# Three sets of expert weights in turn, sample rows first, last sums in the banks

## The reference

```
mix = merged @ w_o
x1  = layer_norm(ALPHA * x + mix)
logits = x1 @ w_group, x1 @ w_router      # top 1 of 4 groups, top 2 of its 8 experts
for each expert e, for the rows routed to it:
    h = silu(xb @ e_gate[e]) * (xb @ e_up[e])
    y = h @ e_down[e]
y = layer_norm(ALPHA * x1 + gate1 * y_first + gate2 * y_second)
```

## Time and profile before

| | us |
|---|---|
| three runs | 1352.65, 1344.41, 1345.07 |
| median | 1345.07 |
| the profiled execution | 1349.2 |
| its span, first to last instruction | 1347.4 |
| TensorE busy | 1120.7 (83%) |
| VectorE busy | 442.2 (33%) |
| ScalarE busy | 238.4 (18%) |
| POOL busy | 113.5 (8%) |

### The profile page before, as it was taken

One profiled execution on the slowest core, in us unless ns is written; L12 is line 12 of the kernel. 1 busy time (PEld: TensorE's weight loads), 2 busy tenths in 40 slices (PEclk: granted clock), 3 DMA queues, 4 the chain that ended last, 5 costly groups with the idle time before them and its releaser, 6 DMA issues.

```text
span 1347.4 us, 21857 instructions
## 1 busy us (share of the span) xinstructions
PE 1120.7 (83%) x9267; PEld 779.1 (58%) x9267; DVE 442.2 (33%) x817; ACT 238.4 (18%) x413; POOL 113.5 (8%) x97
## 2 busy tenths in 40 slices
PE   7999989998989989998999827898878778777730
PEld 4888867777678878876864324444434434444410
DVE  5200013775647657333323262111111111111137
ACT  4000010244321111120101101212111111111101
POOL 0300000000000000000001101111111111111104
PEclk9999999999999999997999958999999999999975
DMA  9432242222221012164454056899999999999941
GB/s 326 134 123 78 68 142 79 63 71 70 55 59 47 27 50 59 26 212 149 169 211 176 32 219 275 365 426 424 424 426 425 423 428 425 425 426 424 414 193 63
DMA packets 48477, 290.82 MB, mean 216 GB/s; under 512 B 9491, under 2 KB 11605, under 8 KB 35594
## 3 DMA queue, kind: packets, MB, share of 16 engines
q1 hardware_dynamic: 43234, 281.41, 53.6%
q0 software_dynamic: 5184, 8.54, 1.7%
HBM read 274.98 MB, written 24.23 MB: 222 GB/s over the span
## 4 chain that ended last, share of the span: by engine, by line
PE 62%; DMA 24%; DVE 6%; ACT 3%; issue 2%; DVEq 2%; POOL 0%; POOLq 0%; SPq 0%; ACTq 0%
PE psum L692 60%; DMA arena<-in_e_up 22%; DVE arena L1477 3%; PE psum L697 2%; ACT arena L1234 2%; DVE arena L1480 2%; DMA arena<-in_p_abm 0%; DMA arena<-in_w_in 0%; DVEq L2099 0%; POOL arena L2112 0%; DVEq L2044 0%; DMA arena<-scratch_x,arena 0%; DMA arena<-in_w_mem_kv 0%; DVE arena L1495 0%; DVEq L1496 0%
## 5 line engine op out<-in xcount | busy, mean ns | idle before, releaser
L692 PE MATMUL psum<-arena 64*64 64x64 f32 (+8 forms) x8760 | 1054.9, 337 | 153.0 <-ACT arena L1234 36.3
L692 PEld LDWEIGHTS psum<-arena 64*64 64x64 f32 (+4 forms) x8760 | 725.3, 151 | 461.6 <-issue 159.4
L1477 DVE TENSOR_TENSOR arena<-arena,psum 128x256 f32<-128x256 f32 (+3 forms) x136 | 74.6, 549 | 504.1 <-PE psum L692 359.5
L1234 ACT ACTIVATE arena<-psum 128x512 f32<-128x512 f32 (+11 forms) x144 | 88.2, 635 | 807.8 <-PE psum L697 413.6
L1477 DVE TENSOR_TENSOR arena<-arena 128x1024 f32<-128x1024 f32 (+17 forms) x168 | 129.8, 784 | 32.6 <-PE psum L692 8.0
L697 PE MATMUL psum<-arena 128*128 128x128 f32 (+5 forms) x507 | 73.9, 279 | 21.3 <-DMA arena<-scratch_x,arena 7.1
L697 PEld LDWEIGHTS psum<-arena 128*128 128x128 f32 (+5 forms) x507 | 54.2, 145 | 53.4 <-issue 31.8
L2112 POOL TENSOR_TENSOR arena<-arena 128x1024 f32<-128x1024 f32 (+1 forms) x15 | 40.9, 2735 | 508.9 <-DVE arena L1477 508.9
L2157 POOL DMA_INDIRECT arena<-scratch_x,arena x32 | 34.0, 1063 | 414.8 <-DVE arena L2060 363.6
L1477 DVE TENSOR_TENSOR arena<-psum,arena 128x256 f32<-128x256 f32 (+4 forms) x85 | 47.1, 565 | 65.7 <-PE psum L692 61.5
L1480 DVE SCALAR_TENSOR_TENSOR arena<-arena 128x520 f32<-128x520 f32 (+7 forms) x72 | 47.1, 667 | 11.1 <-DMA arena<-scratch_ya 7.1
(11 more groups left out here) (111 smaller groups left out, 186.5 us busy)
## 6 DMA issues: line engine op xcount, KB each, us to landing
arena<-in_e_gate SPq DMA_DIRECT2D x32, 2048.0 KB, 26.0
arena<-in_e_up SPq DMA_DIRECT2D x32, 2048.0 KB, 26.5
arena<-in_e_down SPq DMA_DIRECT2D x31, 2048.0 KB, 26.0
arena<-in_w_in SPq DMA_DIRECT2D x46, 512.0 KB, 4.0
scratch_gates<-arena SPq DMA_DIRECT2D x24, 260.0 KB, 4.2
arena<-scratch_gates SPq DMA_DIRECT2D x8, 780.0 KB, 4.7
arena<-in_p_abm SPq DMA_DIRECT2D x8, 640.0 KB, 5.8
scratch_x<-arena SPq DMA_DIRECT2D x8, 512.0 KB
```

The costliest lines, as they stand in the source:

```text
L692: return pe.matmul(out, a, b, start=start, stop=stop)
L1234: return act.activation(out, a, ACT.Copy)
L1477: return v.tensor_tensor(out, a, b, op)
```

## The change

Four edits.

1. Expert weights: sets 0, 1 and 2 take turns for all 32 experts. SP's waits become those of three sets, and its down loads for set 2 are four DMAs. TensorE's loop has six experts in its body instead of two.
2. Output projection: the samples' tile is first (`tile_at` now holds for pas 1 too). Its two halves of 512 columns go to rows 0 to 7 and rows 64 to 71 of bank 0, alternating. VectorE moves the upper half to rows 0 to 7 with one more copy and adds in two operations.
3. The last sums: VectorE scales the identity with each of the two gates for the four prompt tiles (`dg`, eight operations, made before the experts). At the end TensorE puts x1 into all eight banks by products with the identity, and adds the two entries of each row by products with these diagonals. VectorE's statistics and ScalarE's scaling read from the banks. The samples' tile stays on VectorE.
4. The last layer norm's offset moves from POOL to VectorE.

```
-            return (t - 1) % Q if pas == 2 else t
+            return (t - 1) % Q if pas else t
...
-            def gate_load(e, q, done):
-                sp.wait_ge(s["gate_mm"], done + 3)
+            def gate_load(e, q):
+                sp.wait_ge(s["gate_mm"], e)
...
+            def down_load(e, q):
+                sp.wait_ge(s["y_mm"], e)
+                if q < 2:
+                    sp.dma_start(ed[q], one(wd, e)).then_inc(s[f"ew{q}d_in"], 16)
+                else:
+                    for k in range(FF // P):
+                        sp.dma_start(ed2[k], one(wd, e)[:, k, :]).then_inc(s["ew2d_in"], 16)
...
-            gate_load(4, 1, 1)
-            down_load(3, 0, 0)
-            up_load(4, 1, 1)
-            gate_load(5, 0, 3)
-            down_load(4, 1, 1)
-            up_load(5, 0, 3)
-            with sp.Fori(0, NE // 2 - 3) as i:
-                for q in (1, 0):
-                    e = i * 2 + (7 - q)
-                    gate_load(e, q, e - 2)
-                    down_load(e - 1, 1 - q, e - 3)
-                    up_load(e, q, e - 2)
...
+            with sp.Fori(0, NE // 3 - 1) as i:
+                for j in range(3):
+                    e = i * 3 + (4 + j)
+                    gate_load(e, (1 + j) % 3)
+                    down_load(e - 1, j)
+                    up_load(e, (1 + j) % 3)
...
+                    if t == NT:
                         for c in range(KD):
-                            last = mm(bank(2 * (t % 2) + h, 512)[0:n, :], MG[:, c, t * P:t * P + n], wo[h][:, c, :], c == 0, c == KD - 1)
+                            for h in range(2):
+                                last = mm(bank(0, 512)[h * 64:h * 64 + B, :], MG[:, c, T:N], wo[h][:, c, :], c == 0, c == KD - 1)
...
+            with pe.Fori(0, (NE - 2) // 6) as i:
+                for j in range(1, 7):
+                    steady(i * 6 + j, j % 2, i * 3 + j // 2, j % 3, i * 2 + j // 3, (j - 1) % 3, i * 2 + (j - 1) // 3)
...
+            pe.wait_ge(s["route_step"], 4)
+            for t in range(NT):
+                for h in range(2):
+                    mm(bank(2 * t + h, 512), ident, x1[:, t, h * 512:h * 512 + 512], True, False)
+            for t in range(NT):
+                pe.wait_ge(s[f"tile{t}_in"], 32)
+                for h in range(2):
+                    for k in range(2):
+                        last = mm(bank(2 * t + h, 512), dg[:, k, t, :], yk[:, t, k, h * 512:h * 512 + 512], False, k == 1)
+                last.then_inc(s["table_made"], 1)
...
+                if t == NT:
+                    v.tensor_copy(hmove[0:B, :], bank(0, 512)[64:64 + B, :])
+                    v.drain()
+                    stt(x1[0:B, NT, 512:D], x1[0:B, NT, 512:D], ALPHA, hmove[0:B, :], ALU.mult, ALU.add)
+                    stt(x1[0:B, NT, 0:512], x1[0:B, NT, 0:512], ALPHA, bank(0, 512)[0:B, :], ALU.mult, ALU.add).then_inc(s["h_used"], 1)
...
+                        if tail:
+                            v.drain()
+                            tt(x[0:n, i, :], x[0:n, i, :], gb[0:n, 1, :], ALU.add).then_inc(s["x_normed"], 1)
...
+            for k in range(2):
+                for t in range(NT):
+                    ts(dg[:, k, t, :], ident, pgate[:, k, t, :], ALU.mult)
...
+            v.drain()
+            v.sem_inc(s["route_step"], 1)
...
+                if t < NT:
+                    v.wait_ge(s["table_made"], t + 2)
+                    return
...
-            offset(x1, 2)
```

More of the change, by code:

```diff
@@ L616, in _ @@
             sp.dma_start(eg[1], wg[1]).then_inc(s["ew1g_in"], 16)
-            for t in range(Q):
-                sp.wait_ge(s["x_normed"], Q + t + 1)
+            for step in range(Q):
+                t = tile_at(1, step)
+                sp.wait_ge(s["x_normed"], Q + step + 1)
                 sp.dma_start(X["x1"][t * P:t * P + rows(t), :], x1[0:rows(t), t, :]).then_inc(s["x1_spilled"], 16)
@@ L1090, in _, with logits @@
             pe.wait_ge(s["out_in"], 80)
-            def logits(u):
-                pe.wait_ge(s["x1T_ready"], u + 1)
+            def logits(step):
+                u = tile_at(1, step)
+                pe.wait_ge(s["x1T_ready"], step + 1)
                 for c in range(KD):
@@ L1097, in _ @@
             pe.wait_ge(s["gate_out"], N_GATE)
[L1098 to L1103, removed]
-                        for c in range(KD):
-                            last = mm(bank(2 * (t % 2) + h, 512)[0:n, :], MG[:, c, t * P:t * P + n], wo[h][:, c, :], c == 0, c == KD - 1)
+            for step in range(Q + 1):
+                if step < Q:
+                    t = tile_at(1, step)
+                    if step >= 2:
+                        pe.wait_ge(s["h_used"], step - 1)
+                    if t == NT:
+                        for c in range(KD):
+                            for h in range(2):
+                                last = mm(bank(0, 512)[h * 64:h * 64 + B, :], MG[:, c, T:N], wo[h][:, c, :], c == 0, c == KD - 1)
+                    else:
+                        for h in range(2):
+                            for c in range(KD):
+                                last = mm(bank(2 * (step % 2) + h, 512), MG[:, c, t * P:t * P + P], wo[h][:, c, :], c == 0, c == KD - 1)
                     last.then_inc(s["h_made"], 1)
-                if t >= 1:
-                    u = t - 1
+                if step >= 1:
+                    u = tile_at(1, step - 1)
                     n = rows(u)
-                    pe.wait_ge(s["x_normed"], Q + u + 1)
-                    if u >= 1:
-                        pe.wait_ge(s["x1T_ready"], u)
+                    pe.wait_ge(s["x_normed"], Q + step)
+                    if step >= 2:
+                        pe.wait_ge(s["x1T_ready"], step - 1)
                     for c in range(KD):
@@ L1116, in _ @@
                     last.then_inc(s["x1_turned"], 1)
-                if t >= 2:
-                    logits(t - 2)
+                if step >= 2:
+                    logits(step - 2)
             logits(Q - 1).then_inc(s["logits_made"], 1)
@@ L1236, in _, with layer_norm @@
             eps = const("eps")
-            def layer_norm(x, pas, lag, before=None, after=None):
+            def layer_norm(x, pas, lag, before=None, after=None, tail=False):
                 scaled = s["x_scaled" if pas == 0 else "ln_scaled"]
@@ L1250, in layer_norm @@
                         act.wait_ge(s["ln_rs"], pas * Q + u + 1)
-                        act.activation(x[0:n, i, :], x[0:n, i, :], ACT.Identity, bias=nmr[0:n, i, :],
+                        src = bank(2 * i, D) if tail and i < NT else x[0:n, i, :]
+                        act.activation(x[0:n, i, :], src, ACT.Identity, bias=nmr[0:n, i, :],
                                        scale=rstd[0:n, i, :]).then_inc(scaled, 1)
@@ L1493, in layer_norm @@
                         before(i, t)
+                        src = bank(2 * i, D) if tail and i < NT else x[0:n, i, :]
                         for h in range(2):
-                            v.bn_stats(st6[0:n, i, h, :], x[0:n, i, h * 512:(h + 1) * 512])
+                            v.bn_stats(st6[0:n, i, h, :], src[:, h * 512:(h + 1) * 512])
                         v.drain()
```

68 lines of the change are left out of this document (32 added, 36 removed).

## The result

The changed kernel takes 1326.66 us, the median of four runs (1324.38 to 1329.77), against 1345.56 us for the kernel before (four runs, 1344.41 to 1352.65). That is 18.9 us less between the medians; the ratio is 0.9852, with a 95% interval of 0.9818 to 0.9885, or 1.5% faster. The forecast was 1326.3 us, with a range of 1320 to 1338. The sum came out right, but not all of its terms did: the end gave 3.4 us more than forecast, the pieces cost 0.8 us more, the hand-over 0.55 us less, and one edit that was to cost nothing made the stretch behind it 3 us longer.

What follows compares the result with a forecast made beforehand. The prediction took TensorE to bound the projection, the weight stream the experts, and VectorE the end. 6.5 + 3.5 + 10.5 - 0.7 - 1.0 = 18.8 us, from the median 1345.07 to 1326.3 us; range 1320 to 1338.

Steps and rivals of the forecast that it cites:

- the end: After the experts: last sums in the banks by TensorE, offset moved to VectorE; 10.5 us gained.
- the pieces: Expert stream: third set's down weights as four 512 KB loads, nine more experts; 1.0 us lost, bounds 0 and 1.9.
- the hand-over: Before the expert stream: eight identity scalings on VectorE run beside POOL's row gathers; 0.7 us lost, bounds 0 and 1.3.
- projection, alternating halves: Output projection: the samples' two 512-column halves run side by side on TensorE; 6.5 us gained, bounds 0 and 6.6.
- order of the tiles: Output projection: putting the samples' tile first was claimed to give nothing by itself, 0 us.
- hole in the stream: Experts: DMA idle time before expert 5's gate load, filled by the third set; 3.5 us gained, bounds 0 to 3.5.
- The larger copy of its transposes hides behind the logits of the tile before: After the projection: copying the last tile's transposes, now of 128 rows, was claimed to be hidden; no cost counted.
- the rival that the third set returns nothing: Expert stream: the DMA ring finishing last wasn't idle; 3.5 us lost against the forecast, 1329.8 us, chance 0.12.
- The prediction's own main sign: Expert stream: the prediction is wrong above all if the stream of weights takes longer than 467 less 3 us.
- the final store is unchanged: End of the program: the store after the last result was claimed to stay as before; no gain counted.
- The half clock throughout: Rival at the end: TensorE's tile sums run at half clock, 11.7 us after the forecast, 1338 us, chance 0.08.
- the cold first tile: At the end: half clock for the first tile only costs some 2 us and belongs to the forecast.

## Why the prediction was right, and where not

| us | forecast | measured |
|---|---|---|
| projection, alternating halves | +6.5 | +6.8 on TensorE, +7.5 for the whole stretch |
| order of the tiles | 0 | -3.1 (logits) |
| hand-over, diagonals | -0.7 | -0.15 |
| hole in the stream | +3.5 | +3.7 |
| pieces | -1.0 | -1.8 |
| the end | +10.5 | +13.9 |
| routing | 0 | -0.3 |
| sum | 18.8 | 19.8 from landmarks, 18.9 from medians |

**Projection: right.** The price was taken from the 64-row halves of the experts, and 8-row halves behave the same: 7.1 us for eight pairs, where I had 7.3. Of the 7.5 us by which the whole stretch got shorter, 2.1 belong to the order, by the kernel with the samples last.

**"The order itself gives nothing": the step that failed.** Its first half holds, VectorE's operations cost the same for 8 rows. What I wrote of the rest, "The larger copy of its transposes hides behind the logits of the tile before", looked at ScalarE alone. The last tile's transposes and logits are TensorE's, behind the last wait, and there 128 rows cost more than 8: 0.8 us before the logits begin and 2.2 us in them. The row was there, 1.04 us for eight transposes with the shape `8*128 8x8` in the earlier trace rows, and the sentence behind it counted only waits. 2.1 us come back at the product, so that the order as a whole costs 1.5 us (the kernel with the samples last). That the sum came out right all the same is luck: this error of 3.1 us and that of the end, 3.4 us the other way, nearly cancel, and so do the smaller ones (projection +1.0, hand-over +0.5 and hole +0.2 against pieces -0.8 and routing -0.3).

**Hand-over: too dear.** Of 1.3 us, the difference of the two gathers, I charged half to VectorE's presence beside them. The second gather beside the diagonals takes 1.14 us against 1.03 alone, so that presence costs 0.1 us. The first takes 2.30 us in both kernels, each time beside the larger scalings of x1; whether it is long because of them or because it is the first, no run shows.

**Stream: right in its mechanism.** The hole, read from the share of the DMA engines, was 3.5 us and returned 3.7, if the pieces cost what they cost with two sets; the rival that the third set returns nothing is refuted by the stream of the kernel that has it alone (473.64 against 475.67, with the cost of nine sets in pieces in it). For the pieces, of the two rates in the earlier trace rows, that of the stream itself (415 GB/s, 1.9 us) was near, and the mean of both was not. The prediction's own main sign, that it is wrong if the stream takes longer than 467 less 3 us, came true by a little: from the issue of expert 2's up weights to the last up product it is 464.9 us after 466.8. That sign was stricter than the forecast, whose own terms leave 464.3. The Trainium skill (DMA: Bandwidth & Descriptors, section Bandwidth) gives 341 GB/s for a transfer of 1 MB and 425 for one of 16 MB, by which each such set would be 1.2 us dearer, an estimate from that page; its table is of DMAs issued from GpSimd. Here, with SP's loads queued behind each other, it was 0.20 us.

**The end: 3.4 us too small.** 0.8 of it is pace, most of it VectorE's turn of 4.2 us instead of 4.45: I had put 1.55 us for the statistics, 0.35 for reciprocal and product and 2.55 for gain and offset, and from start to start they are 1.49, 0.26 and 2.46 (from 1309.92 us on). The trace of the kernel before has the first two as well, 1.49 and 0.27 from 1314.14 us on. The rest is the sentence "the final store is unchanged". It wasn't: before, 5.75 us passed from the last result to the end of the span, after, 3.1, a difference of 2.65 us. Before, the store's transfer had ended by 1344 and the span at 1347.4, and I hadn't asked what lay between. With the offset off POOL, its last work lies before the last sums, and what follows it no longer sets the end. The half clock throughout didn't occur; the cold first tile did, in two of eight profiles.

## What to carry to other kernels

Read the tail of the profile as well: from each engine's last instruction to the end of the span. Where POOL's is the last, that tail may be longer than the store's, and work taken from POOL at the end gives more than its duration. When tiles change their order, price everything behind the last wait for the tile that is now last, on every engine, TensorE too, and at the clock of that place. A hole in a saturated stream was worth here what the busy share said, less the price of smaller loads, 0.2 us for 2 MB in four pieces.

## What the runs showed of the hardware

- The end of the span follows POOL's last instruction by 5.67 to 5.77 us in seven kernels, and VectorE's, with the store behind it, by 3.0 to 3.1 us in five, in which POOL has been quiet for longer.
- Two products with eight rows each, into rows 0 to 7 and 64 to 71 of one bank, run side by side when their instructions alternate (7.1 us for 16 of 512 columns), and almost one after the other when they don't (12.2; 13.9 with both in one range of rows).
- With three sets, SP's issues themselves grow long. Timeline of SP's queue, changed kernel, at the experts' middle:

```profile
1112.53 0.33 SPq L653 DMA_DIRECT2D arena<-in_e_gate  x1
1118.17 12.33 SPq L665 DMA_DIRECT2D arena<-in_e_down  x4
1130.60 4.50 SPq L657 DMA_DIRECT2D arena<-in_e_up  x1
1135.62 3.77 SPq L653 DMA_DIRECT2D arena<-in_e_gate  x1
```

  In the same stretch of the kernel before each took 0.33 us. More loads are under way (36 us from issue to landing at the median, 26 before), and I take it that an issue waits for room in the queue; no run tested that. I take it that it costs nothing here, although the chain of waits now runs through SP's queue for 4% of the span: the DMA share of the stream is 0.98 as before. SP would be late for anything else behind such a load.
